# Attention's slots rearranged, and two of eight weight pieces of the first modulation multiplied on TensorE

## The reference, cut to what matters

```python
c_act = jax.nn.silu(c)
mod = c_act @ ada_w[i] + ada_b[i]                 # 1024 x 6144
sh1, sc1, gt1, sh2, sc2, gt2 = jnp.split(mod, 6, axis=-1)
h = _modulate(_rmsnorm(x, norm_g[i, 0]), sh1, sc1)
y = _short_conv_mixer(h, conv_w_in[j], conv_w[j], conv_w_out[j])
```

```python
z = jnp.einsum('bhtd,bhsd->bhts', qb, kb) * scale
ls_neg = jax.nn.log_sigmoid(-z)
log_fail = jnp.where(causal, ls_neg, 0.0)
log_rest = lax.cumsum(log_fail, axis=3, reverse=True) - log_fail
att = jnp.where(causal, jnp.exp(z + ls_neg + log_rest), 0.0)
o = jnp.einsum('bhts,bhsd->bhtd', att, vb)
```

## Time and profile before

| What | us |
|---|---|
| median of 3 runs | 3127.62 |
| lowest and highest of them | 3124.7 and 3129.89 |
| the profiled execution, whole | 3128.08 |
| its span, first to last instruction | 3126.3 |
| PE busy in the span | 2929.2 |
| DVE busy | 1552.8 |
| ACT busy | 1054.3 |

### The profile page before, as it was taken

The page is one execution under the profiler, slowest core; times in us unless marked ns, Lnnn a source line. Parts: engine busy times, 40 slices in busy tenths (PEclk is TensorE's granted clock), DMA queues, the critical chain, the costliest instruction groups (busy, mean ns, idle before and its releaser), DMA issues.

```text
span 3126.3 us, 47881 instructions
## 1 busy us (share of the span) xinstructions
PE 2929.2 (94%) x21538; PEld 2364.3 (76%) x21538; DVE 1552.8 (50%) x2187; ACT 1054.3 (34%) x1359; POOL 184.4 (6%) x149
## 2 busy tenths in 40 slices
PE   4999999899999989999899999899999996899999
PEld 3887888678788868888677676678887874578887
DVE  6666554373577644333466666443333665343332
ACT  2225234353233235243432323232222556432221
POOL 1010000101222100000100000000000000000000
PEclk9999999999999999999989999799999998999999
DMA  7554554221000022222211011022323210222321
GB/s 264 185 190 153 189 186 148 85 81 41 16 3 3 17 108 95 94 95 88 71 55 47 36 42 41 28 91 73 115 89 105 81 41 0 74 88 71 120 82 64
DMA packets 41724, 270.18 MB, mean 86 GB/s; under 512 B 4272, under 2 KB 4528, under 8 KB 13360
## 3 DMA queue, kind: packets, MB, share of 16 engines
q1 hardware_dynamic: 39648, 261.39, 23.5%
q10 hardware_dynamic: 1872, 5.74, 0.5%
HBM read 265.01 MB, written 2.10 MB: 85 GB/s over the span
## 4 chain that ended last, share of the span: by engine, by line
PE 86%; DVE 9%; ACT 4%; DMA 1%; issue 1%; POOL 0%; SPq 0%; DVEq 0%; ACTq 0%
PE ps L670 21%; PE ps L671 21%; PE ps L676 21%; PE ps L2083 4%; PE ps L2825 1%; PE ps L2740 1%; PE ps L1631 1%; PE ps L1648 1%; PE ps L1642 1%; PE ps L2731 1%; PE ps L2187 1%; DMA W<-w_ada 1%; PE ps L2156 1%; DVE qk L2360 1%; DVE v L2360 1%
## 5 line engine op out<-in xcount | busy, mean ns | idle before, releaser
L670 PE MATMUL ps<-HH,WH 128*128 128x512 f32 x1928 | 767.8, 398 | 36.6 <-ACT HH L647 35.8
L671 PE MATMUL ps<-HH,WL 128*128 128x512 f32 x1928 | 757.5, 393 | 0.0
L676 PE MATMUL ps<-HL,WH 128*128 128x512 f32 x1928 | 734.6, 393 | 1.7 <-DVE HL L622 1.7
L410 DVE TENSOR_TENSOR WL<-ST,WH 128x2048 fp32r<-128x2048 f32 (+3 forms) x230 | 464.1, 2019 | 254.3 <-ACT WH L402 254.3
L402 ACT ACTIVATE WH<-ST 128x2048 fp32r<-128x2048 f32 (+1 forms) x211 | 383.5, 1818 | 319.0 <-PE ps L676 290.3
L670 PEld LDWEIGHTS ps<-HH,WH 128*128 128x128 f32 x1928 | 367.0, 190 | 122.2 <-issue 45.0
L676 PEld LDWEIGHTS ps<-HL,WH 128*128 128x128 f32 x1928 | 365.8, 190 | 81.7 <-DVE HL L622 4.5
L671 PEld LDWEIGHTS ps<-HH,WL 128*128 128x128 f32 x1928 | 367.1, 190 | 78.4 <-issue 3.1
L670 PE MATMUL ps<-GH,WH 128*128 128x512 f32 x928 | 361.6, 390 | 0.0
L671 PE MATMUL ps<-GH,WL 128*128 128x512 f32 x928 | 361.0, 389 | 0.0
L676 PE MATMUL ps<-GL,WH 128*128 128x512 f32 x928 | 359.8, 389 | 0.0
(11 more groups left out here) (371 smaller groups left out, 3707.7 us busy)
## 6 DMA issues: line engine op xcount, KB each, us to landing
ST<-w_m SPq DMA_DIRECT2D x64, 1024.0 KB, 4.9
ST<-w_gu SPq DMA_DIRECT2D x44, 1024.0 KB, 4.8
ST<-w_ada SPq DMA_DIRECT2D x40, 1024.0 KB, 6.4
ST<-w_dn SPq DMA_DIRECT2D x32, 704.0 KB, 4.0
ST<-w_gin SPq DMA_DIRECT2D x16, 1024.0 KB, 4.8
ST<-w_cin SPq DMA_DIRECT2D x12, 1024.0 KB, 5.1
ST<-w_rkv SPq DMA_DIRECT2D x12, 1024.0 KB, 4.7
ST<-w_kv SPq DMA_DIRECT2D x8, 1024.0 KB, 4.7
```

The source lines that it names most:

```text
L410: o = e.tensor_tensor(WL[:, j % 3, cut], ST[:, pos % 3, cut], WH[:, j % 3, cut].bitcast(F32), ALU.subtract)
L670: e.matmul(ps[:, :], wh[:, k, cs], H[:, k, :], start=(k == 0), stop=False)
L671: e.matmul(ps[:, :], wl[:, k, cs], H[:, k, :], start=False, stop=False)
L676: o = e.matmul(ps[:, :], wh[:, k, cs], L[:, k, :], start=False, stop=(k == kt - 1))
```

## The change

Three edits belong together at the start. DVE now multiplies pieces 0 to 4 whole, then finishes the norm, then multiplies piece 5 in four parts; pieces 6 and 7 it no longer touches. PE multiplies them: for each of 16 output columns, one product with piece 6 and one with piece 7, weights from `W0` and `SM`'s column as the moving operand. They stand ahead of `tensor_columns`, whose products for these blocks no longer begin the sum but add to it.

```
         def tensor_conv(e):
             tensor_rms(e, "conv")
+            for b in flush["first half"] + flush["second half"]:
+                ps = sml.tile(("mod", b))
+                e.wait_ge(*norm_act.at("silu"))
+                e.wait_ge(*sml.free(("mod", b)))
+                for q in range(4):
+                    a = 512 * b + 128 * q
+                    for k in (6, 7):
+                        e.wait_ge(s_ad[k], 16)
+                        e.matmul(ps[:, q:q + 1], W0[:, k, a:a + 128], SM[:, k:k + 1], start=(q == 0 and k == 6),
+                                 stop=False)
             tensor_columns(e, "first half")
...
         def vector_conv(e):
             e.wait_ge(*norm_act.at("silu"))
-            for k in range(7):
+            for k in range(5):
...
+            vector_rms(e, "conv")
+            e.wait_ge(s_ad[5], 16)
+            e.wait_ge(*ada.at("begin", 4))
             for b in flush["first half"] + flush["second half"]:
                 bs = slice(512 * b, 512 * b + 512)
-                e.scalar_tensor_tensor(out=S0[:, bs], in0=W0[:, 7, bs], scalar=SM[:, 7:8], in1=S0[:, bs],
...
-            vector_rms(e, "conv")
```

```
         def tensor_attend(e):
-            for t in range(-1, len(ATTEND) + 3):
+            for t in range(-1, len(ATTEND) + 4):
...
-                for h, j in unit(t - 3):
+                for h, j in unit(t - 4):
                     e.wait_ge(*att_vec.at("weight", h, j))
...
         def scalar_attend(e):
...
+                for h, j in unit(t - 3):
+                    Aw = ATT[h % 4][:, 0:T - P * j]
+                    e.wait_ge(*att_vec.at("log", h, j))
+                    e.activation(Aw, Aw, ACT.Exp).then_inc(*att_act.up("exp", h, j))
                 for h, j in unit(t):
...
-                for h, j in unit(t - 2):
-                    Aw = ATT[h % 4][:, 0:T - P * j]
...
         def vector_attend(e):
...
+                for h, j in unit(t - 1):
+                    w_ = T - P * j
...
                 for h, j in unit(t - 2):
                     w_ = T - P * j
                     e.wait_ge(*att_mm.at("rest", h, j))
...
-                for h, j in unit(t - 1):
-                    w_ = T - P * j
```

More of the change, by code:

```diff
@@ L468, in tensor_columns @@
                 acc = S0[:, 512 * b:512 * b + 512] if b < 4 else ADA[:, b % 2, :]
-                e.wait_ge(*(ada.at("begin", 7, b) if b < 4 else ada.at(2 * b + 1, 3)))
+                e.wait_ge(*(ada.at("begin", 5, b) if b < 4 else ada.at(2 * b + 1, 3)))
                 e.wait_ge(s_tab, 16)
-                e.wait_ge(*sml.free(("mod", b)))
+                if b >= 4:
+                    e.wait_ge(*sml.free(("mod", b)))
                 for q in range(4):
-                    o = e.matmul(ps[:, q:q + 1], acc[:, 128 * q:128 * q + 128], tb("ones")[:, 0:1], start=True,
-                                 stop=True)
+                    o = e.matmul(ps[:, q:q + 1], acc[:, 128 * q:128 * q + 128], tb("ones")[:, 0:1], start=(b >= 4),
+                                 stop=(b >= 4 or q == 3))
                 o.then_inc(*mod_mm.up(b))
@@ L803, in vector_conv @@
                                            op0=ALU.mult, op1=ALU.add).then_inc(*ada.up("begin", k))
-            e.wait_ge(s_ad[7], 16)
-            e.wait_ge(*ada.at("begin", 6))
+            vector_rms(e, "conv")
+            e.wait_ge(s_ad[5], 16)
+            e.wait_ge(*ada.at("begin", 4))
             for b in flush["first half"] + flush["second half"]:
                 bs = slice(512 * b, 512 * b + 512)
-                e.scalar_tensor_tensor(out=S0[:, bs], in0=W0[:, 7, bs], scalar=SM[:, 7:8], in1=S0[:, bs],
-                                       op0=ALU.mult, op1=ALU.add).then_inc(*ada.up("begin", 7, b))
-            vector_rms(e, "conv")
+                e.scalar_tensor_tensor(out=S0[:, bs], in0=W0[:, 5, bs], scalar=SM[:, 5:6], in1=S0[:, bs],
+                                       op0=ALU.mult, op1=ALU.add).then_inc(*ada.up("begin", 5, b))
             vector_low(e, 0)
@@ L2744, in scalar_attend @@
         def scalar_attend(e):
-            for t in range(len(ATTEND) + 4):
+            for t in range(len(ATTEND) + 5):
                 if t == 1:
                     e.wait_ge(*att_vec.at("qq", "normed", 7))
+                for h, j in unit(t - 3):
+                    Aw = ATT[h % 4][:, 0:T - P * j]
+                    e.wait_ge(*att_vec.at("log", h, j))
+                    e.activation(Aw, Aw, ACT.Exp).then_inc(*att_act.up("exp", h, j))
                 for h, j in unit(t):
@@ L2764, in scalar_attend @@
                     e.activation(L, L, ACT.Ln, bias=1.0).then_inc(*att_act.up("ln", h, j))
[L2765 to L2769, removed]
+                for h, j in unit(t - 5):
                     if j == 0:
@@ L2774, in vector_attend @@
         def vector_attend(e):
-            for t in range(len(ATTEND) + 5):
+            for t in range(len(ATTEND) + 6):
+                for h, j in unit(t - 1):
+                    w_ = T - P * j
+                    L, Z = LFT[h % 4][:, OFF[j]:OFF[j] + w_], ZST[h % 4][:, 0:w_]
+                    e.wait_ge(*att_act.at("ln", h, j))
+                    e.scalar_tensor_tensor(out=L, in0=Z, scalar=0.0, in1=L, op0=ALU.max,
+                                           op1=ALU.add).then_inc(*att_vec.up("softplus", h, j))
+                    e.wait_ge(*att_vec.at("softplus", h, j))
+                    e.tensor_tensor(L[:, 0:P], L[:, 0:P], tb("sup"), ALU.mult).then_inc(*att_vec.up("fail", h, j))
+                    e.tensor_tensor(Z[:, 0:P], Z[:, 0:P], tb("sup"), ALU.mult).then_inc(*att_vec.up("masked", h, j))
                 for h, j in unit(t - 2):
@@ L2786, in vector_attend @@
                                            op1=ALU.add).then_inc(*att_vec.up("log", h, j))
[L2787 to L2795, removed]
                 for h, j in unit(t - 3):
@@ L2799, in vector_attend @@
                     e.tensor_tensor(Aw, Aw, tb("sup"), ALU.mult).then_inc(*att_vec.up("weight", h, j))
-                for h, j in unit(t - 5):
+                for h, j in unit(t - 6):
                     if j == 0:
```

## The result

The changed kernel takes 3088.64 us (median of 4 runs, 3086.99 to 3089.61), the kernel before 3126.16 (4 runs, one more than ahead of the prediction). The ratio is 0.988, 95% interval 0.9863 to 0.9897: faster by 37.5 us, 1.2%. 3095 was predicted, in a range of 3084 to 3108, so the forecast held and was 6.4 us too high. The profiled execution took 3088.98 with a span of 3087.2, against 3128.08 and 3126.3: 39.1 less.

What follows compares the result with a forecast made beforehand. PE bounds the kernel almost everywhere, except for DVE's chain at the start and a loop closing once per slot in attention. Profiled 3128.1 + 8.4 (start) - 41.2 (attention) = 3095.3, predicted as 3095, range 3084 to 3108.

Steps and rivals of the forecast that it cites:

- The start, +8.4: At the start, 31 products and eight sums queue on PE behind piece 7's landing, delaying the first scaled input 8.4 us.
- The rival of full clock: At the start, PE's products speed up to 0.198 us after 3.5 us, costing only 0.8 us: 3088 in all; 12%.
- Attention, -41.2: In attention, the fullest engine instead of a one-slot loop sets each slot: stage 80.5 us instead of 121.75.
- the allowance for half clock: In attention, 2 us added to the 78.5 us stage for stretches where PE runs at half clock.
- The head outputs: In attention, they come a slot later, costed at nothing; uncovered, one narrow slot of 1.3 us.
- The reading of the loops: In attention, a loop closed once per slot before (5.18 us at j = 0); after, each takes two slots or more.
- the two loops named: One-slot attention loops foretold for single edits: rest, log, softplus, fail, rest (4.0 us); rest, log, mask, o, rest (4.2 us).
- The rival of a loop that still closes in one slot: In attention, DVE waiting for Ln holds back the log that ACT's Exp needs; gain only 6.5 us, 3130 in all; 6%.
- The two rivals of half clock in attention: PE at half clock in part of attention (3102 to 3110; 16%) or through all of it (3156; 4%).

Runs made afterwards that it cites:

- the run with ten wide products: The changed kernel with ten idle products of 512 columns on PE between the norm's sums and the products of one column: 3086.41 us, ratio 0.9866 to before.
- piece 6 alone: The changed kernel, but PE multiplies only piece 6 and DVE adds piece 7 last: 3081.38 us, ratio 0.9846 to the kernel before.
- the two single edits: In the kernel before, only PE's o one slot later (3095.1 us, ratio 0.9891), or only DVE's softplus ahead of log (3094.3 us, ratio 0.9896).
- the half-by-half kernel: The changed kernel with piece 6 and 7 products for blocks 3 and 1 behind the sums for blocks 2 and 0: 3083.56 us, ratio 0.9843 to before.

## Why the prediction was right

Its two main terms were right in mechanism and nearly so in size.

**The start, +8.4.** The landing of piece 7 was forecast at 34.8 and came at 34.58; 0.437 a product was 0.432. The first scaled input stood at 51.68 instead of 52.3 to 52.4: 7.7 late instead of 8.4. PE's next columns at 72.17 were foretold at 72.9. Less than this is left behind the wait. Before, the clock was at half for 6.9 us there; in the changed kernel it fell later, and the eight passes took 1.05 instead of 1.87:

```profile
73.50:77.00 3.50, 3.50 (x10) 2.76 (x9) 2.97 (x3) 0.95 (x2) 0.00 (x0) 0.52 0.79 307
```

The dense products go on at 73.22, which was 66.38, so the changed kernel is 6.8 late from there. That the loss reaches the end is shown by the pair with and without the new start: 3088.64 against 3080.99, and 3137.53 against 3128.74.

**The rival of full clock** gave 3088, where the time is, and is false all the same. It let the clock rise after 3.5 us of such products, which no run here shows: all 31 ran at 0.432, and in the run with ten wide products a raised clock fell while they ran. By the Trainium skill (TensorE: Matmul & The Clock Gate, "Why this matters for your kernels") TensorE that is kept busy goes to full clock. The trace disagrees for products of one column: PE was busy with them from 34.58 to 54.8 without a break, and the 16 sums at the end still took 0.436 each. The dense products behind them took 0.43 until 59.8 and 0.23 from there. (The view's clock column reads 1.00 there, without a record; with piece 6 alone it reads 0.50 from 30 to 45, at the same price.) A time that agrees with a rival's is not evidence for it: its mark was a first scaled input before 45.

**Attention, -41.2.** This is the term that was mis-sized most, by 3.8 us. The stage took 76.7 instead of 80.5. Of this 2.0 was the allowance for half clock: after 2596 there was none, and ahead of it, at j = 3, the chain runs through ACT. The other 1.8 is what errors of the slots leave when they cancel, which is luck. I gave each slot the price of its fullest engine with units of one width, but a slot holds z, rest and o of units of different j. So the slots of j = 0 are 3.67, 3.02 and 3.24 instead of 3.9: an o of j = 1 (0.65) or a z of j = 3 stands beside the rest of j = 0. The second four of j = 3 are longer than the 1.3 foretold. The head outputs, a term put at nothing, stand in the chain of ACT there:

```profile
2628.55 0.17 ACT ZS L2772
...
2629.57 0.49 ACT HH L2783
2630.05 0.20 ACT AT L2762
2630.25 0.17 ACT ZS L2772
```

This slot is 1.70, and 0.49 of it is the head output. (The 2.8 for ACT at j = 0 takes 0.53 for a Ln whose row has 0.63; PE sets those slots, so the forecast does not move.) The reading of the loops is shown by the two single edits: each left exactly one of the two loops named, at 4.13 and 4.05 us a slot.

**The sum again**, by the profiled executions, whose difference is 39.1. Attention was entered 7.3 late (2590.76 and 2583.50) where 8.4 was forecast; it gave 45.0 where 41.2 was; and 1.3 us more came behind it, which I had at nothing. 1.1 + 3.8 + 1.3 = 6.2, which is the 6.3 that the forecast of 3095.3 is above 3088.98, but for rounding. The 1.3 is the clock at one place that the change does not touch: behind attention PE waits 5.32 us in both kernels and goes on with dense products at half clock, for 6.1 us before and for 3.4 us now. Before, and then now:

```profile
2756.70:2762.80 6.10, 6.10 (x15) 4.76 (x16) 5.96 (x9) 2.88 (x5) 0.00 (x0) 0.50 0.01 3
```

```profile
2718.90:2722.30 3.40, 3.37 (x8) 2.72 (x9) 3.31 (x5) 1.70 (x3) 0.00 (x0) 0.51 0.00 0
```

2.7 us less at half clock are 1.3 us of time. That the two middles came out within 0.4 us of each other, in the table above, is luck too.

**The rival of a loop that still closes in one slot** (3130) is out. ACT's Exp (2762) waits for log (2804) 8 us in all, six times, in the list of waits; 2779 is Ln, 2791 softplus, 2794 fail:

```profile
DVE LF L2791 <- ACT LF L2779: 10.5, 22, 1.0
DVE AT L2804 <- PE ps L2751: 10.2, 8, 2.1
ACT AT L2762 <- DVE AT L2804: 8.0, 6, 2.2
...
PE ps L2751 <- DVE LF L2794: 3.0, 6, 0.9
```

(engine and line, waited for: us in all, times, longest.) None of these occurs in all 32 slots, as a wait in a one-slot loop would. The two rivals of half clock in attention are out as well: after 2596 there was none.

## What to carry to other kernels

Where engines hand one unit to each other in turn, write down for each order of steps which steps close a loop within one slot; as long as one does, its sum sets the slot's length here, and no engine's load does. Two edits that each break a part of it did not add up. Work moved from a loaded engine to an idle one did not pay here while it stood behind the last arrival: count what is queued between that arrival and the first result somebody waits for. And read a small gain at a place just behind the edit, not only in the whole time, when the part behind it varies by more.

## What the runs showed of the hardware that was not expected

- TensorE's clock fell from 1.00 to 0.50 with PE busy all the time on products of one column (37.0 above, at half clock to 57.5), from 0.11 us a pass to 0.216.
- Runs of one kernel differ by the clock in a stretch that the change does not touch. Between 1630 and 1900 us (delta rule) PE does some 2400 narrow passes. In the changed kernel the clock fell there five times (from about 1633, 1685, 1739, 1794 and 1848); in the profiled run of the half-by-half kernel it stayed at 1.00 to 1879. Stretches of these two, one each:

```profile
1630.00:1900.00 270.00, 261.45 (x2392) 187.26 (x2390) 167.53 (x358) 81.92 (x125) 9.98 (x10) 0.95 0.12 40
```

```profile
1620.00:1880.00 260.00, 251.23 (x2401) 178.72 (x2399) 169.93 (x362) 82.46 (x125) 10.01 (x10) 1.00 0.12 42
```

Nearly the same number of instructions takes 10 us less at 1.00 than at 0.95. (0.95 on average means that a tenth, 27 us, went at half clock, which costs 13.5 at most.) The program there is the same. The profiled run of piece 6 only (3073.15, where its three others are at 3080.9 to 3081.9) missed one of these falls, 1.00 from 1690 to 1745 against 0.93 in the changed kernel. That the moment at which the stretch begins decides it is my guess: the runs of one kernel fell on both sides (3068.6 and 3087.2), and no run here moved the moment alone. It stays open. It also means that the few us between 3075 and 3081 are medians with such runs among them.
